# Six separate walks instead of one interleaved plan for the dilated attention

## What is computed

```
qb, kb, vb = slices of proj            # proj = h @ w_in
logits = einsum(q, k) * hd**-0.5 + bias    # keys within +-64 dilated steps
lse    = logsumexp(where(mask, logits, NEG))
o_g    = einsum(exp(logits - lse), v)
# later: softmax over the three lse, weighted sum of the three o_g
```

## Time and profile before

| | us |
|---|---|
| median of 3 runs | 3333.54 |
| lowest and highest | 3332.79, 3345.88 |
| the profiled execution, whole | 3333.54 |
| its span in the profile | 3331.7 |
| TensorE busy | 3135.6 |
| VectorE busy | 1498.5 |
| ScalarE busy | 1054.1 |

### The profile page before, as it was taken

One profiled execution on the slowest core, in us unless ns is written; L12 is line 12 of the kernel. 1 busy time (PEld: TensorE's weight loads), 2 busy tenths in 40 slices (PEclk: granted clock), 3 DMA queues, 4 the chain that ended last, 5 costly groups with the idle time before them and its releaser, 6 DMA issues.

```text
span 3331.7 us, 38836 instructions
## 1 busy us (share of the span) xinstructions
PE 3135.6 (94%) x16207; PEld 2555.2 (77%) x16207; DVE 1498.5 (45%) x2115; ACT 1054.1 (32%) x2293; POOL 361.3 (11%) x433
## 2 busy tenths in 40 slices
PE   7999999898899998999989999999999999998998
PEld 4788888777777876877744788888888886777887
DVE  4556556665653123131123345444444567631453
ACT  3544444444332222232300132221221233212453
POOL 0222232232221000000010000000000011000211
PEclk9999999999999999999999999999999999998899
DMA  2211111111101101101352411111111230111101
GB/s 106 65 57 45 45 51 45 32 32 39 32 29 60 64 32 45 53 30 48 125 202 69 155 63 59 48 51 51 51 51 51 83 104 26 51 38 45 37 29 39
DMA packets 59313, 194.86 MB, mean 58 GB/s; under 512 B 7649, under 2 KB 15329, under 8 KB 49410
## 3 DMA queue, kind: packets, MB, share of 16 engines
q1 hardware_dynamic: 58272, 191.29, 16.6%
q10 hardware_dynamic: 866, 1.09, 0.1%
HBM read 158.37 MB, written 33.98 MB: 58 GB/s over the span
## 4 chain that ended last, share of the span: by engine, by line
PE 80%; DVE 10%; ACT 6%; issue 2%; DMA 1%; POOL 0%; ACTq 0%; SPq 0%; DVEq 0%; POOLq 0%
PE ps L2307 18%; PE ps L2309 18%; PE ps L2308 17%; PE ps L2006 5%; PE ps L2184 3%; PE ps L701 3%; PE ps L707 3%; PE ps L1682 2%; PE ps L3144 1%; PE ps L744 1%; PE ps L3203 1%; DVE ar L1102 1%; PE ps L752 1%; PE ps L753 1%; PE ps L1647 1%
## 5 line engine op out<-in xcount | busy, mean ns | idle before, releaser
L2307 PE MATMUL ps<-r,r 128*128 128x512 f32 (+2 forms) x2656 | 1047.5, 394 | 40.4 <-DVE r L228 10.3
L2309 PE MATMUL ps<-r,r 128*128 128x512 f32 (+2 forms) x2656 | 996.2, 375 | 0.0
L2308 PE MATMUL ps<-r,r 128*128 128x512 f32 (+2 forms) x2656 | 993.8, 374 | 0.0
L2307 PEld LDWEIGHTS ps<-r,r 128*128 128x128 f32 x2656 | 507.5, 191 | 134.0 <-issue 17.2
L2309 PEld LDWEIGHTS ps<-r,r 128*128 128x128 f32 x2656 | 504.5, 190 | 93.9
L2308 PEld LDWEIGHTS ps<-r,r 128*128 128x128 f32 x2656 | 507.6, 191 | 80.1 <-issue 5.0
L2307 PE MATMUL ps<-r 128*128 128x512 f32 x512 | 199.6, 390 | 0.8 <-DVE r L2300 0.8
L2309 PE MATMUL ps<-r 128*128 128x512 f32 x512 | 199.2, 389 | 0.0
L2308 PE MATMUL ps<-r 128*128 128x512 f32 x512 | 199.2, 389 | 0.0
L2557 DVE TENSOR_TENSOR ar<-ar,ps 128x512 f32<-128x512 f32 x224 | 151.0, 685 | 92.2 <-PE ps L2309 92.1
L2006 PE MATMUL ps<-ar 128*128 128x512 f32 x384 | 170.9, 604 | 8.6 <-DMA ar<-sc_o 6.5
(11 more groups left out here) (321 smaller groups left out, 4322.4 us busy)
## 6 DMA issues: line engine op xcount, KB each, us to landing
ar<-wst SPq DMA_DIRECT2D x76, 1024.0 KB, 4.8
ar<-wst SPq DMA_DIRECT2D x52, 512.0 KB, 3.9
ar<-x SPq DMA_DIRECT2D x16, 512.0 KB, 9.9
ar<-sc_g SPq DMA_DIRECT2D x32, 256.0 KB, 4.8
sc_h<-ar SPq DMA_DIRECT2D x32, 256.0 KB, 2.2
sc_x<-ar SPq DMA_DIRECT2D x16, 512.0 KB, 2.8
ar<-sc_x SPq DMA_DIRECT2D x16, 512.0 KB, 4.1
sc_b<-ar SPq DMA_DIRECT2D x24, 260.0 KB, 2.0
```

What stands on the lines that cost most here:

```text
L2307: t.do.matmul(o, l[0], r[0], start=first, stop=False)
L2308: t.do.matmul(o, l[0], r[1], start=False, stop=False)
L2309: return t.do.matmul(o, l[1], r[0], start=False, stop=last)
```

## The change

The one merged list becomes six lists, walked one after the other: v 0 alone; att 0 with v 1; qk 1 alone; att 1 with v 2; qk 2 alone; att 2 with gb. In the three pairs both threads run over the same scale (0 to 1), so their steps are spread evenly. No instruction is added or removed. In the new file each line behind the plan is one higher (L1647 is L1648, and so on).

```diff
-        plan_dil = [merged((("v", 0), 20, 0.0, 44.0), (("att", 0), 34, 36.0, 148.0), (("v", 1), 20, 44.0, 136.0),
-                           (("qk", 1), 33, 134.0, 228.0), (("att", 1), 34, 227.0, 348.0), (("v", 2), 20, 228.0, 335.0),
-                           (("qk", 2), 33, 333.0, 425.0), (("att", 2), 34, 424.0, 492.0), (("gb", 3), 17, 424.0, 490.0))]
+        plan_dil = [[("v", 0)] * 20,
+                    merged((("att", 0), 34, 0.0, 1.0), (("v", 1), 20, 0.0, 1.0)), [("qk", 1)] * 33,
+                    merged((("att", 1), 34, 0.0, 1.0), (("v", 2), 20, 0.0, 1.0)), [("qk", 2)] * 33,
+                    merged((("att", 2), 34, 0.0, 1.0), (("gb", 3), 17, 0.0, 1.0))]
```

## The result

The changed kernel takes 3358.82 us (median of 6 runs, 3351.47 to 3362.62), the kernel before 3336.98 us in the same comparison (3332.79 to 3345.88). The ratio is 1.0053, with a 95% interval of 1.0036 to 1.007: slower, by 18 us as the ratio has it (the two medians differ by 21.8) where 6 were forecast, and 9 us past the end of the range. Executions of one and the same kernel lie 11 to 13 us apart here, so the reasons are read from the profiles, stage by stage, and the verdicts from the ratios. The profiled executions, 3333.54 and 3351.55 us, are 18.0 us apart too; both lie near the fast end of their kernel.

The account below looks back on a forecast made before the run. PE bounds the kernel; the planned stretch loses 38.5 us to its waits and 17.3 to half clock. Waits +2.2 and clock +4 gave +6 us on 3333.54, 3339.5 rounded to 3339 us; range 3328 to 3350.

Parts of the forecast that it names:

- 4.8 + 16.2: First group with v 1: PE waits of 4.8 us at the head (-1.5) and 16.2 us after U0 (+1.2).
- forecast 16.6: Second group with v 2: PE waits rise from 10 to 16.6 us, +6.5, the largest term.
- the turn behind exp 7: First group: a wait of 5.7 us becomes 2.9, since one half block now lies between.
- +2.2 us: All three groups: the changes in PE waits together, -1.5 + 1.2 + 6.5 - 4.0.
- At the same rate that is 8.75 stretches, 1.75 x 2.5 = +4 us: Clock term: ten gaps of about 2 us and more, eight before, give 8.75 half-clock stretches instead of seven, +4 us.
- clock cascade: Rival, second group, 1413 to 1514: each gap pulls the clock down in long stretches; +17 us, 3351 us, chance 0.09.
- Its condition of 13 stretches: The number of half-clock stretches from which the cascade rival was to decide.
- What spoke against it: Argument against the cascade rival: two other gaps ahead of half blocks, 1.75 us each, had no half-clock stretch.
- The rule that was weighed: Skill rule on the clock ramp: by it the clock term is dropped, +2.2, 3335.7 us; the prediction kept the term.
- -4.0: Third group with gb: PE waits fall from 7.3 to 3.3 us as the gaps of 0.67 us go.
- I cost it at nothing: SP's order: stores of a group's last tiles now issued ahead of the next stage's weight loads; cost taken as nothing.

Follow-up runs that it names:

- tune1: The kernel before with one merged list of other begin and end numbers, the qk stages beginning earlier; 3305.55 us against 3340.14, ratio 0.9898.
- second_cut: The kernel before with att 1 and v 2 cut off as a list of their own, old spacing kept; 3341.36 us against 3340.14, ratio 1.0007.
- third_loads: only_third with the two 1 MB weight loads issued right behind a store; 3331.09 us against 3340.14, ratio 0.9972.
- before_loads: The kernel before with its weight loads issued right behind a store, as a control; 3339.68 us against 3338.32, ratio 1.0004.
- only_third: The kernel before with the new order in the third group alone (att 2 with gb); 3338.1 us against 3339.06, ratio 0.9999.

## Why the prediction was wrong

**The waits of the first two groups were right, gap by gap.** First group: forecast 21.0 us (4.8 + 16.2), measured 20.6. Second: forecast 16.6 (the terms as listed add up to 16.1), measured 15.9, with 2.38 us ahead of U10, 1.56 ahead of U8, 1.52 ahead of U15, 2.74 and 2.76 ahead of two turns; the turn behind exp 7 waited 2.76 us instead of 5.74 (2.9 forecast). In all +2.2 us were forecast and +4.8 measured; the difference is mostly the third group's.

**The step that failed is the clock: "At the same rate that is 8.75 stretches, 1.75 x 2.5 = +4 us".** It measured 12.5 us, with twelve stretches in all: that much longer PE is busy on the same matmuls (449.3 us in the three stages against 436.8), and nearly all of it in the second group, which has six stretches instead of one. The term counted only gaps of about 2 us and more and gave each the same chance. Neither holds:
- Shorter gaps counted. In the changed kernel 1.56 us (U8), 1.52 (U15) and 1.42 with 0.60 behind it were each followed by half clock, and so was 1.12 with 0.85 behind it at the head of the third group, where none was forecast. Another gap of 1.42, ahead of the half block after T9, was not.
- Longer ones did not always. The first group has seven gaps of 1.99 to 3.07 us and only four stretches: those of 2.18, 1.99 and 2.07 were followed by none. In the second all three were followed.

The rows tied stretches to gaps nearly one to one because they came from one profile. In others of the same order the same gap is followed by half clock or not, as shown in the section on the result. So a rate from one profile could not carry this term. What decides in a given execution these runs do not settle. The size was off as well, by less: the second group's stretches were 5.6 us on average and full of matmuls, so each cost 2.8 us, not 2.5.

**The rival "clock cascade"** (0.09) named the place, 1413 to 1514, and the five gaps: U8, U10, two turns and U15 were each followed by half clock. Its size is right in part by luck. Its condition of 13 stretches did not come (12 in all, of 3.4 or 6.8 us in this group and not 10.1), it had 15 us for the clock instead of 12.5 and 2.2 for the waits instead of 4.8; its 3351 us is what the profiled execution took (3351.55). What spoke against it, the two gaps of 1.88 and 1.69 us without a stretch, was luck of the profile for the first of them: in the four other kernels with the old order it had one. The second had none in any.

**The rule that was weighed.** The Trainium skill, "TensorE: Matmul & The Clock Gate", section "What's actually happening", says that the ramp is under 1% of a typical span, varies between runs and should not be fitted. By it the term could have been dropped, and the forecast would have been further off, since the clock was two thirds of the loss. That it varies between runs the traces bear out. Under 1% they do not for the execution as a whole: its mean granted clock is 0.974 before and 0.971 after, 2.6 and 2.9% below full.

The Trainium skill, "Perfetto Trace Analysis", section "Optimization Strategy", says that interleaving stages with different limits may help. The traces agree as far as tune1 goes, which overlaps neighbouring stages more and is 1% faster than the kernel before; of the loss of this change second_cut puts only a part down to the cuts (ratio 1.0007 against 1.0053; 4 of 15 us in the profiles).

**The third group: "-4.0" became 0.** Its gaps went as forecast (3.3 us without the store's 4.0). "I cost it at nothing", said of SP's order, failed. I had looked at SP for loads that come too late, not for loads that hold up a store behind them, and no wait on a store stood in the earlier trace rows, since it is DVE that waits for it. third_loads and before_loads show both sides: the wait appears where the next tile's store follows the loads by 2 us (the changed kernel, only_third, tune1), not where it follows by 7 to 8.

**Sum.** Waits +4.8 and longer busy time +12.5: 17.3, the stretch's growth in the profiles. The half clock accounts for the second: 64.9 us of it against 41.0, with 62.2 and 35.0 us of PE's work in it (summed over the stretches of both traces), of which half is lost: 13.6 us by this estimate. Of the 20 us between 3339 and the median of 3358.82, 3.4 are the kernel before itself, whose median was 3333.54 in three runs and 3336.98 in six.

## What to carry to other kernels

Judge a reordering by the gap time and the work that is done slowly after it, both. For the second count no length of gap decided here: one of 1.12 us with 0.85 behind it was followed by half clock, one of 2.75 was not. So leave none of these out, take the rate from several profiles and not from one, and give the term a wide range. When a step moves, look at each queue that it shares for what now stands just behind a large transfer, and at waits of every engine that feeds the critical one. Where a stage waits on its own chain, start the next stage's independent work there rather than sort the stages apart, as tune1 did (along with a new spacing; which of the two gained how much was not separated).

## What was not expected of the hardware

A gap of 1.5 us between matmuls was followed by 6.7 us at 1.2 GHz in a dense stage, and one and the same gap of 1.87 to 1.88 us, in the same order of work, by none in one kernel and by 3.4 us in five others. Adding 46 unneeded matmuls made the stage 11.7 us faster. And a store of 260 KB behind two loads of 1 MB on the same queue landed after 6.5 us, three times its usual 2.0.
